# Fewer columns in the weight-stationary matmuls of expert items with up to 136 rows

## The reference, cut to what matters

```python
def moe_swiglu(h, w_router, w1, w3, w2):
    ...
    top_logit, top_e = lax.top_k(logits, TOP_K)
    ...
    def expert_block(args):
        xb, e = args
        return (jax.nn.silu(xb @ w1[e]) * (xb @ w3[e])) @ w2[e]
```

## Time and profile before

| | |
|---|---|
| median of 3 executions | 2060.63 us |
| profiled execution, its own time | 2059.9 us |
| its span, first to last instruction | 2058.2 us |
| PE busy | 1979.8 us (96%) |
| DVE busy | 1567.9 us (76%) |
| ACT busy | 1101.3 us (54%) |
| HBM traffic over the span | 219 GB/s |

### The profile page before, as it was taken

One profiled execution on the slowest core, in us unless ns is written; L12 is line 12 of the kernel. 1 busy time (PEld: TensorE's weight loads), 2 busy tenths in 40 slices (PEclk: granted clock), 3 DMA queues, 4 the chain that ended last, 5 costly groups with the idle time before them and its releaser, 6 DMA issues.

```text
span 2058.2 us, 34371 instructions
## 1 busy us (share of the span) xinstructions
PE 1979.8 (96%) x12246; PEld 1755.2 (85%) x12247; DVE 1567.9 (76%) x1964; ACT 1101.3 (54%) x1269; POOL 91.3 (4%) x104
## 2 busy tenths in 40 slices
PE   7999999999989999999999999999999999999993
PEld 6889887878779788999999988788999888999882
DVE  6866535353567586888888899998888998888996
ACT  5532433232335423555655577777555776555773
POOL 0000000000000001200100010100000101000101
PEclk9999999999999999999999999999999999999997
DMA  5312623232322214777777799999777999776983
GB/s 196 103 62 93 259 89 102 82 102 82 112 72 83 76 58 151 258 245 258 269 244 267 251 362 373 363 377 358 263 260 245 335 378 334 252 266 236 378 318 145
DMA packets 218812, 450.44 MB, mean 219 GB/s; under 512 B 13217, under 2 KB 64433, under 8 KB 218769
## 3 DMA queue, kind: packets, MB, share of 16 engines
q1 hardware_dynamic: 210416, 421.05, 58.6%
q0 software_dynamic: 8352, 28.80, 3.7%
HBM read 432.23 MB, written 17.58 MB: 219 GB/s over the span
## 4 chain that ended last, share of the span: by engine, by line
PE 83%; DVE 10%; issue 3%; ACT 2%; DMA 1%; DVEq 0%; POOL 0%; ACTq 0%; SPq 0%; POOLq 0%
PE ps L583 18%; PE ps L585 17%; PE ps L584 17%; PE ps L925 12%; PE ps L942 8%; PE ps L927 5%; PE ps L944 3%; DVE w_lo L1777 2%; DVE w_lo L1774 1%; PE ps L652 1%; ACT w_hi L1189 1%; DVE ex L1356 1%; DVE w_lo L1331 1%; PE ps L846 1%; ACT w_hi L1191 0%
## 5 line engine op out<-in xcount | busy, mean ns | idle before, releaser
L1774 DVE TENSOR_TENSOR w_lo<-raw,w_hi 128x1024 fp32r<-128x1024 f32 x340 | 415.4, 1222 | 81.4 <-ACT w_hi L1189 78.9
L925 PE MATMUL ps<-xt,w_hi 128*128 128x304 f32 x1792 | 457.1, 345 | 2.7 <-DVE xt L1788 2.3
L927 PE MATMUL ps<-xt,w_lo 128*128 128x152 f32 x1792 | 420.0, 234 | 0.0
L1189 ACT ACTIVATE w_hi<-raw 128x1024 fp32r<-128x1024 f32 x340 | 357.5, 1052 | 107.6 <-PE ps L927 56.9
L1777 DVE TENSOR_TENSOR w_lo<-raw,w_hi 128x1024 fp32r<-128x1024 f32 x340 | 415.0, 1221 | 0.0
L1191 ACT ACTIVATE w_hi<-raw 128x1024 fp32r<-128x1024 f32 x340 | 356.3, 1048 | 0.0
L927 PEld LDWEIGHTS ps<-xt,w_lo 128*128 128x128 f32 x1792 | 343.0, 191 | 0.1
L925 PEld LDWEIGHTS ps<-xt,w_hi 128*128 128x128 f32 x1792 | 338.8, 189 | 3.3 <-issue 3.2
L583 PE MATMUL ps<-act_hi,w_hi 128*128 128x512 f32 x608 | 242.0, 398 | 5.5 <-DVE act_lo L1375 5.5
L585 PE MATMUL ps<-act_hi,w_lo 128*128 128x512 f32 x608 | 239.9, 395 | 0.0
L584 PE MATMUL ps<-act_lo,w_hi 128*128 128x512 f32 x608 | 239.8, 394 | 0.0
(11 more groups left out here) (330 smaller groups left out, 3164.8 us busy)
## 6 DMA issues: line engine op xcount, KB each, us to landing
raw<-in_moe_w_dram SPq DMA_DIRECT2D x672, 512.0 KB, 5.2
raw<-in_w_in_dram SPq DMA_DIRECT2D x19, 1024.0 KB, 5.1
raw<-in_ffn_w_gate_dram SPq DMA_DIRECT2D x11, 1024.0 KB, 5.4
raw<-in_ffn_w_up_dram SPq DMA_DIRECT2D x11, 1024.0 KB, 5.3
raw<-in_ffn_w_down_dram SPq DMA_DIRECT2D x11, 1024.0 KB, 4.9
raw<-in_w_out_dram SPq DMA_DIRECT2D x8, 1024.0 KB, 4.9
y_rows<-mult POOLq DMA_DIRECT2D x1, 8192.0 KB, 29.5
y_rows<-yacc POOLq DMA_DIRECT2D x8, 512.0 KB, 5.2
```

The costliest lines, as they stand in the source:

```text
L925: pe.matmul(pairs_of(ps[:, bank, 0:2 * NW]), hi_[:, k % 4, f * P:(f + 1) * P], xt[:, k, :, 0:NW], start=k == 0, stop=False)
L927: last = pe.matmul(ps[:, bank, NW:2 * NW], lo_[:, k % 4, f * P:(f + 1) * P], xt[:, k, 0, 0:NW], start=False, stop=k == KT - 1)
L1189: act.activation(slot_hi[p % 6][:, 0:half], raw6(p)[:, 0:half], ACT.Copy).then_inc(w_hi_half, 1)
L1774: dve.tensor_tensor(slot_lo[p % 6][:, 0:half], raw6(p)[:, 0:half], f32(slot_hi[p % 6][:, 0:half]), ALU.subtract)
```

## The change

A third form is added. The DVE sets the flag to 2 where a turned item has at most NARROW = 136 rows (136 - 2·128 = -120 is what is compared with rows minus 128 times blocks), with two more small instructions in its chain. On PE, a turned item of form 2 runs its six loop iterations with pairs of 272 and 136 columns, in a loop of its own; chunk 0's gate and up, the last down, and everything that ACT and DVE do stay at 152 rows. The tiles keep their places: 272 columns are two stretches of 136 with 16 left out between them, in the moving operand and in PSUM.

```diff
 NW = P + 24
+NARROW = P + 8
...
-            def turned_up(kind, f, p, c_at):
+            def turned_up(kind, f, p, c_at, nw=NW):
...
-                    pe.matmul(pairs_of(ps[:, bank, 0:2 * NW]), hi_[:, k % 4, f * P:(f + 1) * P],
-                              xt[:, k, :, 0:NW], start=k == 0, stop=False)
-                    last = pe.matmul(ps[:, bank, NW:2 * NW], lo_[:, k % 4, f * P:(f + 1) * P],
-                                     xt[:, k, 0, 0:NW], start=False, stop=k == KT - 1)
+                    pe.matmul(pairs_of(ps[:, bank, 0:2 * NW])[:, :, 0:nw], hi_[:, k % 4, f * P:(f + 1) * P],
+                              xt[:, k, :, 0:nw], start=k == 0, stop=False)
+                    last = pe.matmul(ps[:, bank, NW:NW + nw], lo_[:, k % 4, f * P:(f + 1) * P],
+                                     xt[:, k, 0, 0:nw], start=False, stop=k == KT - 1)
...
-            def turned_down(d, p, c_at):
+            def turned_down(d, p, c_at, nw=NW):
...
-                    pe.matmul(pairs_of(ps[:, bank, 0:2 * NW]), hi_[:, f % 2, d * P:(d + 1) * P],
-                              ht_n[:, f, :, :], start=f == 0, stop=False)
-                    last = pe.matmul(ps[:, bank, NW:2 * NW], lo_[:, f % 2, d * P:(d + 1) * P],
-                                     ht_n[:, f, 0, :], start=False, stop=f == 3)
+                    pe.matmul(pairs_of(ps[:, bank, 0:2 * NW])[:, :, 0:nw], hi_[:, f % 2, d * P:(d + 1) * P],
+                              ht_n[:, f, :, 0:nw], start=f == 0, stop=False)
+                    last = pe.matmul(ps[:, bank, NW:NW + nw], lo_[:, f % 2, d * P:(d + 1) * P],
+                                     ht_n[:, f, 0, 0:nw], start=False, stop=f == 3)
...
-            def item_turned(n):
+            def turned_chunks(n, nw):
+                with pe.Fori(0, EC - 1) as c:
...
+            def item_turned(n, form):
...
-                with pe.Fori(0, EC - 1) as c:
...
+                with pe.If(form > 1):
+                    turned_chunks(n, NARROW)
+                with pe.Else():
+                    turned_chunks(n, NW)
...
             with pe.Fori(0, n_items) as n:
-                with pe.If(pe.snap(turned_next, min_val=0, max_val=1) > 0):
-                    item_turned(n)
+                form = pe.snap(turned_next, min_val=0, max_val=2)
+                with pe.If(form > 0):
+                    item_turned(n, form)
                 with pe.Else():
                     item_one(n)
...
             link(dve.tensor_tensor(w3v[3], n_row, over_n(last_item), ALU.is_equal))
+            link(dve.scalar_tensor_tensor(rest_of, rest_of, float(NARROW - 2 * P), turned_e, ALU.is_le, ALU.mult))
+            link(dve.tensor_tensor(turned_e, turned_e, rest_of, ALU.add))
             link(dve.tensor_tensor(w3v[3], w3v[3], over_n(turned_e), ALU.mult))
```

More of the change, by code:

```diff
@@ L949, in turned_down @@
                     last.then_inc(y_ps, 1)
-            def item_turned(n):
+            def turned_chunks(n, nw):
+                with pe.Fori(0, EC - 1) as c:
+                    q, at_ = n * EC + c, n * IP + c * 6
+                    for f in range(4):
+                        if f % 2 == 0:
+                            pe.wait_ge(gs_ready, q * 2 + (f // 2 + 1))
+                            pe.wait_ge(y_added, q * 4 + (f // 2 + 3))
+                        turned_up(0, f, 4, at_, nw)
+                    for f in range(4):
+                        if f % 2 == 0:
+                            pe.wait_ge(us_ready, q * 2 + (f // 2 + 1))
+                        turned_up(1, f, 6, at_, nw)
+                    pe.wait_ge(ht_lo_done, q * 2 + 2)
+                    for d in range(KT):
+                        if d % 2 == 0:
+                            pe.wait_ge((us_ready, gs_ready)[d // 4], q * 2 + (3 + d % 4 // 2))
+                        turned_down(d, 8, at_, nw)
+            def item_turned(n, form):
                 pe.wait_ge(xt_lo_done, n * 2 + 2)
@@ L1309, in _ @@
             with act.Fori(0, n_items) as n:
-                turned_form = act.value_load(items[0:1, bass.ds(n + 48, 1)], min_val=0, max_val=1)
+                turned_form = act.value_load(items[0:1, bass.ds(n + 48, 1)], min_val=0, max_val=2)
                 with act.If(turned_form > 0):
@@ L2009, in _ @@
             with dve.Fori(0, n_items) as n:
-                turned_form = dve.value_load(items[0:1, bass.ds(n + 48, 1)], min_val=0, max_val=1)
+                turned_form = dve.value_load(items[0:1, bass.ds(n + 48, 1)], min_val=0, max_val=2)
                 with dve.If(turned_form > 0):
```

## The result

The changed kernel takes **2124.09 us** (median of 5 executions, 2121.15 to 2128.7), against 2060.63 before: ratio 1.0308, 95% interval 1.0296 to 1.032. It is 3% slower where 0.4% faster was forecast. The profiled execution took 2121.15 us.

A forecast was written before the change was run, and what follows sets the result against it. PE was taken to set the pace, with DVE close behind in the turned items. Terms -8.3 + 0.4 + 0.3 = -7.6 us put the median at 2053.0 us, against 2060.6 before; range 2049.5 to 2057.5.

The forecast's parts named there:

- A pair saves 14 ns: PE's matmul pairs in the narrow loop: only the long half gains, 140 to 126 ns; bounds nothing to 21 ns.
- Items 1 and 4 are narrow: Of the turned items, these two have 136 rows each, exactly the limit; items 0 and 6 stay wide.
- Rival 2: Routing by rounding leaves only one item narrow: 4.1 us gained, 2057.2 us; chance 8%.
- The ring: DVE's unchanged chain holds PE at down d = 2, so a narrow iteration takes 23.50 us instead of 24.26.
- Rival 1: DVE's chain shortens with PE, so PE's pace alone counts: 14.1 us gained, 2047.2 us; chance 7%.
- 8.3 us for two items: Gain of the narrow loops: 0.34 us in the first iteration and 0.76 in each of five more, per item.
- Two DVE instructions, 0.4 us: Added to DVE's chain for the list of items, which PE's first pair waits for; uncovered, +0.41 us.
- An If on PE in every turned item: A branch ahead of the loop and a jump behind it, mostly covered by waits: 0.3 us in all, bounds 0 and 1.5.
- Rival 4: Taken branches around the turned items' loops fetch code: eight at 2.17 us, 17.4 us, time 2070.1 us; chance 3%.
- Its loop jumping back over 384 instructions shows no gap: Argument against slow code fetching: PE's loop in the turned items jumps back each time without a visible gap.

The follow-up runs named there:

- e5: Changed kernel with PE's item loop moved by 152 instructions, through a never-true If ahead of it; 2058.79 us, ratio 0.9993.
- e7: e5 with, on DVE, the second half of piece 11's rest moved behind the last hidden value; 2052.15 us, ratio 0.9964.
- e3: Changed kernel without the If, its one loop always of 272 and 136 columns, leaving out rows of two experts; 2046.56 us, ratio 0.9923.
- e4: Kernel before the change plus an If in the turned item whose never-run side holds 100 transposes, some 200 instructions; 2065.16 us, ratio 1.0029.
- e6: Changed kernel with PE's item loop moved by 52 instructions, through a never-true If ahead of it; 2062.31 us, ratio 1.0014.
- e8: Changed kernel with PE's item loop moved by 232 instructions, through a never-true If ahead of it; 2119.02 us, ratio 1.0283.
- e1: Changed kernel with the second loop's matmuls back at 304 and 152 columns, both loops and the If kept; 2129.11 us, ratio 1.0333.
- e2: Changed kernel without its two DVE instructions, so the narrow loop is there but never runs; 2126.84 us, ratio 1.0322.
- e10: e7 with the wide loop placed ahead of the narrow one; 2054.36 us, ratio 0.9973.

## Why the prediction was wrong, point by point

- **A pair saves 14 ns: right.** Pairs start 0.238 us apart (0.253 before, 0.239 forecast). The start of the short half after the long one fell from 0.182 to 0.174 us and the next pair's from 0.071 to 0.064, as means of some 40 pairs; the sum is what the line through 256 and 512 columns gave.
- **Items 1 and 4 are narrow: right**; the page by forms has 768 + 384 matmuls of 272 columns. Rival 2 is out.
- **The ring: right.** L1907 starts 1085.30 - 1068.11 = 17.19 us after the iteration's start (17.21 forecast), d = 2 at 17.71 (17.73), the iteration takes 23.46 (23.50), and PE waits 0.4 us ten times. The wait, over all of a turned item's down products, grew to 8.0 us, not to 11: those of items 0 and 6 were swallowed by stalls, a wait's idle time is shorter than the distance of starts, and the two first iterations wait 0.8 us longer (0.4 at d = 0, 1.4 at d = 2), not 1.0. In e5, where only item 0's is swallowed, it is 9.0. Rival 1 is out: the ring stands until the move of e7.
- **8.3 us for two items: right in the changed kernel.** The six iterations of items 1 and 4 take 142.4 us each, against 146.8 and 146.7 before: 8.8 together. In e5 item 1 gained 4.4 and item 4 only 2.7, since there the clock fell behind the longer waits of its first iteration, as in e3. The prediction had no term for that; it costs 1.6 us where it comes.
- **Two DVE instructions, 0.4 us: not settled.** The first pair came 0.9 us later, and it moves by some 4 us between the profiled executions of these kernels (828.5 in e7, 832.8 in e3, both with the two instructions).
- **"An If on PE in every turned item", 0.3 us, at most 1.5: this step failed.** The chip showed about 70 us (its span is 61.3 us longer, and that is after the 8.8 that the narrow loop gained). I priced the If as a branch, by the 0.37 us of an item's start, and bounded it with that row times four. That row was itself measured in a loop that stays loaded. The If is cheap (e4), but the 400 instructions behind it are not: they took the loop from about 1240 to 1640 instructions and, with the start of the loop that e5, e6 and e8 give, from 6 blocks to 8. The row that would have told is the queue of instructions: 29 packets before, none after item 1's start at 1007 us. I read only gaps and never asked why there was nothing to fetch.
- **Rival 4, slower by fetching code, named the right cause with the wrong place and price.** It counted eight taken branches at 2.17 us. The stalls were eight, but of 1.8 to 11.9 us, and the large ones are not at the new branches but at the items' ends, where the loop goes on to the next item. "Its loop jumping back over 384 instructions shows no gap" was no evidence: it showed that a loop that fits is not fetched again, which is just what the change ended. The Trainium skill's rule that the prediction cites ("Runtime: NRT & Kernel Launch", section "Instruction fetch mechanics"), that a taken branch outside the loaded window must fetch, agrees with these stalls. The same section puts that window at two blocks; e5, whose loop of 7 blocks jumps back without a stall from item 1 on, does not agree. I let the absence of a stall in the kernel before speak against the rule.
- **The clock behind a stall** had no term. It adds about 2 us to seven of the eight (granted clock 0.50 for 3 to 7 us after PE goes on).

With the position mended (e5) the sum would be -8.3 + 0.4 + 6 once, -1.9 us; measured are -0.7 (medians) and -1.3 (the part behind the first pair): the first jump over unloaded code takes most of the gain even then, and item 4's spell of slow clock another 1.6.

## What to carry to other kernels

Before adding a second body to a loop, count the instructions of the whole loop on that engine, and look at the packets of the instruction queue: if none fall in the loop now, the loop lives in the engine's memory, and the first question about a change is whether it still does. Where the edge is near, move the loop by a few dozen instructions and time it again before judging the idea. Bound an added branch by a fetch of all that the loop holds, not by the cheapest branch in the trace.

## What the chip showed that was not expected

- PE's loop of about 1640 instructions is fetched once when it lies on 7 blocks of 256 (e5, e6: 31 packets in all) and again in every turned item when it lies on 8 (the changed kernel, e1, e2, e8: 60 or 61 packets). The step between the two costs 60 us of 2060. That the number of blocks is the cause is inferred from four positions of the same code; the contents of the engine's memory were not seen.
- The fetches cost little in the middle of straight code, where some lie beside running matmuls, and 11 to 12 us at the end of a turned item, where PE jumps over the other side and back to the loop's start.
- A first jump over a body that is not yet loaded costs 3.0 to 4.8 us once from start to start (e4, e5, e6, e7, e10), then nothing. It does not always: the kernel before goes on after 0.37 us of idle time at item 0's end.
- Behind two waits of 0.4 and 1.4 us in a narrow item's first iteration the granted clock fell to 0.50 for some 3 us in 6 of 12 items, 1.6 us each; in the wide items of the kernel before and of e4, with one wait of 1.0 to 1.3 us there, in none.
- Running the `item_one` side again and again (items 2 and 3) fetched nothing even in the kernel that was over the limit.
